# Hybrid encoder block on one core: nine matmuls of `zv` moved behind the first step of `za`, the row scale moved ahead by one table step, and the load order changed to match

## The reference, cut to what matters

```python
def _rms(x, g):
    y = xf * lax.rsqrt(jnp.mean(xf * xf, axis=-1, keepdims=True) + EPS)
    return (y * g.astype(jnp.float32)).astype(x.dtype)
...
h = _rms(x, g_mix[l])
z = h @ w_in[l]
za, zu, zv, zq, zg = jnp.split(z, SPLITS, axis=-1)
ya = jax.nn.gelu(_s5(za, ...))
yb = _sgu(zu, zv, ...)
yc = _mem_xattn(zq, mem, ...)
merged = gates[:, :, 0] * ya + gates[:, :, 1] * yb + gates[:, :, 2] * yc
x = x + merged @ w_out[l]
```

## Time and profile before

| | |
|---|---|
| median of 3 runs | 768.78 us (768.48 to 768.9) |
| the profiled execution's own time | 768.33 us |
| its span in the profile | 766.6 us |
| TensorE busy | 758.3 us, 99% of the span |
| VectorE, ScalarE, GpSimd busy | 552.5, 355.4, 314.6 us |
| mean granted TensorE clock | 0.999 of full speed |

### The profile page before, as it was taken

How to read it: one execution, slowest core, us unless ns; L and a number is a source line. 1 busy time by engine, 2 the same in 40 slices (tenths; PEclk the granted TensorE clock), 3 DMA queues, 4 the chain that set the end, 5 groups by cost and what they waited for, 6 DMA issues and landing times.

```text
span 766.6 us, 9762 instructions
## 1 busy us (share of the span) xinstructions
PE 758.3 (99%) x3562; PEld 629.0 (82%) x3562; DVE 552.5 (72%) x752; ACT 355.4 (46%) x529; POOL 314.6 (41%) x169
## 2 busy tenths in 40 slices
PE   8999999999999999999999999999999999999997
PEld 7788887788888888888888888888888888888886
DVE  6999997684848484246767787777787677836687
ACT  6796567643535333634343423232323333434554
POOL 4456655233333333444444444444444354830000
PEclk9999999999999999999999999999999999999999
DMA  7744333022222443222233866666668567768853
GB/s 273 301 147 131 117 98 112 30 91 83 81 85 68 126 144 104 83 93 100 83 111 99 272 196 228 217 217 191 201 204 285 176 218 228 264 229 279 293 201 125
DMA packets 42371, 126.17 MB, mean 165 GB/s; under 512 B 4192, under 2 KB 6368, under 8 KB 40544
## 3 DMA queue, kind: packets, MB, share of 16 engines
q1 hardware_dynamic: 42192, 125.45, 49.1%
q10 hardware_dynamic: 144, 0.26, 0.1%
HBM read 107.08 MB, written 18.61 MB: 164 GB/s over the span
## 4 chain that ended last, share of the span: by engine, by line
PE 91%; ACT 3%; DVE 3%; DMA 1%; issue 1%; SPq 0%; POOL 0%; ACTq 0%
PE bank L1641 24%; PE bank L1643 24%; PE bank L1642 24%; PE bank L2005 4%; PE bank L2007 4%; PE bank L2006 4%; ACT uc L656 1%; DVE s5p L1015 1%; PE bank L1882 1%; PE bank L1757 1%; PE bank L1774 1%; DMA xT<-xt_dram 1%; ACT w_hi L596 1%; DVE tab_tmp L1015 1%; DVE h_lo L1020 1%
## 5 line engine op out<-in xcount | busy, mean ns | idle before, releaser
L535 POOL TENSOR_TENSOR w_lo<-raw,w_hi 128x1024 fp32r<-128x1024 f32 x90 | 218.1, 2424 | 300.7 <-ACT w_hi L596 300.7
L596 ACT ACTIVATE w_hi<-raw 128x1024 fp32r<-128x1024 f32 x112 | 118.8, 1060 | 310.9 <-PE bank L1643 306.3
L1641 PE MATMUL bank<-h_hi,w_hi 128*128 128x512 f32 x608 | 238.5, 392 | 0.2 <-POOL w_lo L540 0.2
L1643 PE MATMUL bank<-h_hi,w_lo 128*128 128x512 f32 x608 | 236.7, 389 | 0.0
L1642 PE MATMUL bank<-h_lo,w_hi 128*128 128x512 f32 x608 | 236.6, 389 | 0.0
L1641 PEld LDWEIGHTS bank<-h_hi,w_hi 128*128 128x128 f32 x608 | 114.2, 188 | 24.3 <-issue 1.0
L1643 PEld LDWEIGHTS bank<-h_hi,w_lo 128*128 128x128 f32 x608 | 114.1, 188 | 23.9
L1642 PEld LDWEIGHTS bank<-h_lo,w_hi 128*128 128x128 f32 x608 | 114.2, 188 | 23.7 <-issue 0.5
L540 POOL TENSOR_TENSOR w_lo<-raw,w_hi 128x512 fp32r<-128x512 f32 x48 | 67.2, 1420 | 52.4 <-ACT w_hi L596 46.0
L1015 DVE TENSOR_TENSOR mix<-mix 128x512 f32<-128x512 f32 x44 | 47.6, 1083 | 13.1 <-DMA mix<-w_dram 11.9
L1015 DVE TENSOR_TENSOR lo<-raw,hi 128x1536 fp32r<-128x1536 f32 (+1 forms) x19 | 32.8, 1732 | 24.8 <-ACT hi L925 24.6
(11 more groups left out here) (328 smaller groups left out, 1384.6 us busy)
## 6 DMA issues: line engine op xcount, KB each, us to landing
raw<-w_dram SPq DMA_DIRECT2D x112, 512.0 KB, 3.4
mix<-w_dram SPq DMA_DIRECT2D x11, 1024.0 KB, 8.0
mix_dram<-mix SPq DMA_DIRECT2D x11, 1024.0 KB, 6.3
raw<-w_dram SPq DMA_DIRECT2D x30, 256.0 KB, 4.3
raw<-mix_dram SPq DMA_DIRECT2D x26, 256.0 KB, 3.8
half_dram<-odd SPq DMA_DIRECT2D x11, 256.0 KB, 8.3
second<-half_dram SPq DMA_DIRECT2D x3, 768.0 KB, 6.0
raw<-mix_dram SPq DMA_DIRECT2D x3, 768.0 KB, 4.2
```

The source lines that it names most:

```text
L535: nc.gpsimd.tensor_tensor(w_lo[:, s, :], raw[:, s, :], fv(w_hi[:, s, :]), ALU.subtract).then_inc(w_ready, 1)
L596: nc.scalar.activation(w_hi[:, slot, :], raw[:, slot, :], ACT.Copy).then_inc(w_rounded, 1)
L1641: mm(out, a[0], b[0], start=first, stop=False)
L1643: return mm(out, a[1], b[0], start=False, stop=last)
```

## The change

The first 512 columns of `zv`'s first weight tile (tile 4, which is one of its two steps) are loaded once more, into a buffer `raw_v` of their own, right after `x`'s first tile. ScalarE rounds them to `v_hi` behind `x`'s first tile, GpSimd subtracts them to `v_lo` behind the first half of weight tile 0, and TensorE does the nine matmuls of `zv_step(0, range(3))` behind `za_step(0)` instead of behind `za_step(7)`. Tile 4 is still loaded and rounded as a whole. In SyncE's order tile 4 now stands ahead of the fourth token tile, tile 5 ahead of `mtok`; ScalarE rounds tile 4 ahead of the fourth token square. On VectorE `x_scale` comes behind `table_step(1)`, and the copy to `rstd` ahead of `table_step(4)`; `uT` stays behind both. Some semaphores are shared (`diag`, `wide_done`, `trig_ready`).

```diff
+        raw_v = at("raw_v", o_f + 2048, [P, WB])
+        v_hi = at("v_hi", o_f + 4096, [P, WB], R)
+        v_lo = at("v_lo", o_f + 6144, [P, WB], R)
...
             for k in range(4):
                 load_first(k // 2, k % 2)
                 load_x(k)
+                if k == 0:
+                    sp.dma_start(raw_v[:, :], w_d[T_ZV, :, 0:WB]).then_inc(v_loaded, 16)
             load_x(4)
             next_weights(2)
             load_x(5)
             next_weights(3)
-            for t in range(4):
+            for t in range(3):
                 sp.dma_start(xtok[:, t, :], xtok_d[:, t, :]).then_inc(xtok_loaded[t], 16)
             next_weights(4)
+            sp.dma_start(xtok[:, 3, :], xtok_d[:, 3, :]).then_inc(xtok_loaded[3], 16)
             sp.dma_start(memf[:, :, :], mem_d).then_inc(mem_loaded, 16)
             sp.dma_start(small[:, C_BRE:N_SMALL], small_d[:, C_BRE:N_SMALL]).then_inc(small_loaded, 16)
+            next_weights(5)
             sp.dma_start(mtok[:, :, :], mtok_d).then_inc(mtok_loaded, 16)
-            for t in range(5, 8):
+            for t in range(6, 8):
                 next_weights(t)
...
                     low_half(t, j).then_inc(done, 1)
+                    if t == 0 and j == 0:
+                        pool.wait_ge(v_rounded, 1)
+                        nc.gpsimd.tensor_tensor(v_lo[:, :], raw_v[:, :], fv(v_hi[:, :]), ALU.subtract
+                                                ).then_inc(v_ready, 1)
...
                 round_first(k // 2, k % 2)
                 round_x(k)
+                if k == 0:
+                    act.wait_ge(v_loaded, 16)
+                    nc.scalar.activation(v_hi[:, :], raw_v[:, :], ACT.Copy).then_inc(v_rounded, 1)
...
             for t in range(4):
+                if t == 3:
+                    round_weights(T_ZV)
                 act.wait_ge(xtok_loaded[t], 16)
                 token_square(xtok, t, t)
             act.wait_ge(tok_sq, 4)
             root(tstd[:, :], tssq[:, 0:4]).then_inc(tok_std, 1)
-            round_weights(T_ZV)
...
-            def table_step(n, scale=None):
+            def table_step(n):
...
-                if scale:
-                    scale()
                 turn_squared(ER, EI, ER, EI)
...
             table_step(1)
-            table_step(2, x_scale)
+            x_scale()
+            table_step(2)
+            dve.wait_ge(wide_done, 1)
+            V.tensor_copy(rstd[:, :], bank[7][:, :]).then_inc(rstd_ready, 1)
             table_step(4)
-            dve.wait_ge(wide_x, 1)
-            V.tensor_copy(rstd[:, :], bank[7][:, :]).then_inc(rstd_ready, 1)
             dve.wait_ge(rstd_ready, 1)
...
-            for k in range(KD):
+            za_step(0)
+            x_hi, x_lo = h(0)
+            pe.wait_ge(v_rounded, 1)
+            for c in range(3):
+                mm(bank[4 + c][:, :], x_hi[:, c * P:(c + 1) * P], v_hi[:, :], start=True, stop=False)
+            for c in range(3):
+                mm(bank[4 + c][:, :], x_lo[:, c * P:(c + 1) * P], v_hi[:, :], start=False, stop=False)
+            pe.wait_ge(v_ready, 1)
+            for c in range(3):
+                mm(bank[4 + c][:, :], x_hi[:, c * P:(c + 1) * P], v_lo[:, :], start=False, stop=False)
+            for k in range(1, KD):
                 za_step(k)
...
-            pe.wait_ge(w_half, T_ZV + 1)
-            zv_step(0, range(3))
-            pe.wait_ge(diag_x, 1)
-            wide_rows(7, xdiag[:, :, :], T, wide_x)
+            pe.wait_ge(diag, 1)
+            wide_rows(7, xdiag[:, :, :], T, wide_done)
```

More of the change, by code:

```diff
@@ L265, in build @@
         w_used = sem("w_used")
+        v_loaded, v_rounded, v_ready = sems("v_loaded v_rounded v_ready")
         X_PARTS = ((0, 1), (1, 2), (2, 3), (3, 4), (4, 6), (6, 8))
@@ L277, in build @@
         norms = {n: dict(zip(keys, sems(" ".join(f"{n}_{k}" for k in keys)))) for n, keys in NORM_KEYS.items()}
-        tok_sq, tok_std, diag_x, diag_m, wide_x, wide_m, rstd_ready, mrstd_ready = sems(
-            "tok_sq tok_std diag_x diag_m wide_x wide_m rstd_ready mrstd_ready")
+        tok_sq, tok_std, diag, wide_done, rstd_ready, mrstd_ready = sems(
+            "tok_sq tok_std diag wide_done rstd_ready mrstd_ready")
         za_taken, zv_taken, zq_taken, k_taken, v_taken, zu_scaled, zu_ready = sems(
@@ L286, in build @@
         pt_done, pt_act, pt_dve, pv_done, o_hi_s, o_lo_s = sems("pt_done pt_act pt_dve pv_done o_hi_s o_lo_s")
-        dt_ready, ang_ready, trig_ready = sems("dt_ready ang_ready trig_ready")
+        ang_ready, trig_ready = sems("ang_ready trig_ready")
         j1_g, j1_th, j1_merge = sems("j1_g j1_th j1_merge")
@@ L623, in _ @@
             act.wait_ge(vec_loaded, 16)
-            nc.scalar.activation(s5p[:, 0, :], small[:, C_LDT:C_LDT + 16], ACT.Exp).then_inc(dt_ready, 1)
+            nc.scalar.activation(s5p[:, 0, :], small[:, C_LDT:C_LDT + 16], ACT.Exp).then_inc(trig_ready, 1)
             for k in range(4):
@@ L1027, in _ @@
             dve.wait_ge(vec_loaded, 16)
-            dve.wait_ge(dt_ready, 1)
+            dve.wait_ge(trig_ready, 1)
             go(tt(XR, are, DT, ALU.mult))
@@ L1048, in _ @@
                 low_x(k)
-            dve.wait_ge(trig_ready, 1)
+            dve.wait_ge(trig_ready, 2)
             go(tt(ARE, MAG, CS, ALU.mult))
@@ L1129, in x_scale @@
             def x_scale():
-                token_scale(4, 1, tstd[:, :], trstd[:, :], xdiag[:, :, :], diag_x)
+                token_scale(4, 1, tstd[:, :], trstd[:, :], xdiag[:, :, :], diag)
             table_step(1)
-            table_step(2, x_scale)
+            x_scale()
+            table_step(2)
+            dve.wait_ge(wide_done, 1)
+            V.tensor_copy(rstd[:, :], bank[7][:, :]).then_inc(rstd_ready, 1)
             table_step(4)
-            dve.wait_ge(wide_x, 1)
-            V.tensor_copy(rstd[:, :], bank[7][:, :]).then_inc(rstd_ready, 1)
             dve.wait_ge(rstd_ready, 1)
@@ L1144, in _ @@
                 low_tile(norms["m"], m_hi, m_lo, memf, C_GMEM, k)
-            token_scale(2, 2, mtstd[:, :], mtrstd[:, :], mdiag[:, :, :], diag_m)
+            token_scale(2, 2, mtstd[:, :], mtrstd[:, :], mdiag[:, :, :], diag)
             bre, bim, cre, cim = (grid(c0) for c0 in (C_BRE, C_BIM, C_CRE, C_CIM))
@@ L1173, in _ @@
             times([c[:, 0, :, :] for c in cpow], (cre, cim), ARE, AIM, True, 1)
-            dve.wait_ge(wide_m, 1)
+            dve.wait_ge(wide_done, 2)
             V.tensor_copy(mrstd[:, :], bank[3][:, 0:M]).then_inc(mrstd_ready, 1)
@@ L1729, in _ @@
                 if t == 3:
-                    pe.wait_ge(diag_m, 1)
+                    pe.wait_ge(diag, 2)
                     pe.wait_ge(za_taken, KB)
-                    wide_rows(3, mdiag[:, :, :], M, wide_m)
+                    wide_rows(3, mdiag[:, :, :], M, wide_done)
                 for j in range(2):
```

## The result

The change makes the kernel 0.24% slower: 770.48 us (median of 22 runs, 769.35 to 771.74) against 768.64 us for the kernel before (22 runs, 767.87 to 769.99). The ratio is 1.0024, with a 95% interval of 1.0018 to 1.0030, so about 1.8 us more.

The account below looks back on a forecast made before the run. Bound at the start, where TensorE's matmuls meet VectorE's uT followed by ScalarE at 61.42 us. A 2.1 us hold makes uT late: 768.33 + 2.1 = 770.4 profiled, plus 0.45 to the median, so 770.9 us; range 768.0 to 772.2.

Parts of the forecast that it names:

- Two paths, the later decides: At 61.42 us TensorE's matmuls meet VectorE up to uT followed by ScalarE; the later one sets the time.
- ScalarE's stretch from `uT` to the half rest: ScalarE's work from 36.91 to 59.5 has no idle stretch; if it got shorter, late uT would not reach TensorE.
- tile 5's pair: GpSimd's two subtractions for tile 5, expected to start at about 33.5, where they were.
- The hold of 2.1 us: VectorE's table step 4, behind rstd, held by GpSimd's pair for tile 5: 2.1 us, bounds 0 to 2.56; chance 0.62.
- The added load: v's extra 256 KB slice behind x's first tile: no shift taken, VectorE at most 0.64 us later.
- The table step did not get by: First rival: the third table step ends before GpSimd's pair or runs beside none, uT not held, 768.3 to 768.8; chance 0.32.
- The fourth token row: Rival: this row lands at 30.8 behind tile 4, delaying the root and uT by 4.2 us, total 773.0; chance 0.06.
- The moved matmuls did find something to fill: Third rival denied it: v's slice lands with x's second tile, TensorE's 0.7 us is lost, total stays 770.9; no chance given.
- the 0.9 that I gave its path: TensorE's path up to 61.42 becomes 0.9 us shorter: 0.7 from the moved matmuls plus 0.2 of idle.
- The 0.7 us: TensorE's gain from the moved matmuls: through at 30.3 instead of 31.03.
- The wait ahead of 61.42: TensorE's idle time before the half rest at 61.42, taken as 0.2 us.
- 771.3: The total by the skill page's blocking rule, each subtraction holding VectorE for its whole length: 768.78 + 2.56.

Follow-up runs that it names:

- e1: The changed kernel with only table_step(4) moved behind the four uT: 768.41 us against 768.56 for the kernel before, ratio 0.9997.
- e5: The kernel before, with the copy of rstd and the four uT put ahead of table_step(4): 768.56 us against 768.59, ratio 1.0003.
- e6: The changed kernel with VectorE's old order (scale behind table_step(2), copy of rstd behind table_step(4)): 769.23 us, ratio 1.0015 to the kernel before.
- e4: The changed kernel with token rows and tile 4's rounding in the old order and table_step(4) behind uT: 767.47 us against 768.56 before, ratio 0.9986.
- e0_change_a: The changed kernel, unaltered, run once more for another profile: 769.63 us, one execution.

## Why the prediction was right

**Two paths, the later decides.** Right, and shown from both sides: with `uT` late the time follows it one for one (the table), with `uT` early TensorE's own path is met (e1, e5). ScalarE's stretch from `uT` to the half rest kept its length, 22.7 us (37.90 to 60.62, 36.91 to 59.58 in the earlier trace rows); it was the point on which everything could have failed.

**The terms.** Predicted and measured, in the first profile of the change:

| step | predicted | measured |
|---|---|---|
| nine matmuls | 9.23 to 11.27 | 9.23 to 11.29 |
| TensorE through `za` | 30.3 | 30.48 (30.65 less 0.17 idle) |
| tile 3 rounded from | 19.5 | 19.70 |
| tile 4 rounded from | 24.9 | 25.14 |
| fourth token square from | 26.1 | 26.83 |
| `tok_std` | 28.9 | 29.6 |
| tile 5's pair from | 33.5 | 33.93 |
| copy of `rstd` done | 32.65 | 32.75 |
| table step behind it, hold | 2.1 | 1.0 (1.1 and 2.1 in the two other executions) |
| last `uT` done | 39.0 | 37.9 (38.2 and 39.2) |

ScalarE's rows behind the second half of the table:

```profile
25.14 1.06 ACT L609 ACTIVATE w_hi<-raw 128x1024 fp32r<-128x1024 f32 x1 [1.26 <-PE bank L1715]
26.83 1.06 ACT L631 ACTIVATE xtok<-xtok 128x1024 f32<-128x1024 f32 x1 [0.62 <-DMA xtok<-xtok_dram]
...
29.29 0.30 ACT L618 ACTIVATE tstd<-tssq,eps 128x4 f32<-128x4 f32 x1
...
32.81 1.05 ACT L609 ACTIVATE w_hi<-raw 128x1024 fp32r<-128x1024 f32 x1
```

The fourth square waits 0.62 us for its row, which I had put at 25.9 and which came at 26.8. In the two other executions the square starts at 26.22 and 26.12, as predicted. The late row passes on to the root, but not to `rstd`: by the sum itself VectorE came to the scale only at 29.4, 0.5 us behind the root. It idled 0.29 us there and made most of it up in the scale and table step 2.

**The mis-sized term.** The hold of 2.1 us, taken from the earlier trace rows, is right for an execution in which both of GpSimd's subtractions catch the step, and twice too large where only one does. In three profiles it was 1.0, 1.1 and 2.1. The prediction had one held subtraction only as the low end of its range. Which case comes up follows the start of tile 5's pair (33.93 and 34.36: one; 33.25: two), and that follows ScalarE's eight `m_hi`: they began at 29.59 and 30.02, in the first case behind the late row, in the second after waiting 1.04 us for the memory's rows, and at 28.92 in the third. So the execution whose token and memory rows came most punctually lost the most. The 22 runs lie between 769.35 and 771.74, where one and two holds (+1.0 and +2.1 on 768.64) would put most of them. The median, 770.48, lies near the execution with two holds (770.60), and only one of the 22 is below the second execution with one (769.63). That each timed run has one or two holds is an inference, since only three were traced. Of the 0.4 us by which 770.9 is too high, 0.14 is the base (768.78 from three runs, 768.64 from 22); the rest is this term, 1.84 in the medians for 2.1.

**The added load.** Taken at nothing, with a bound of 0.64 us. `h_hi` of `x`'s second tile started at 8.64, 8.54 and 9.30 in the three executions (8.73 before), so in one of them 0.6 us late. Nearly all of that was made up on the way: the copy of `rstd` started at 32.06, 32.26 and 32.30.

**The rivals.** The table step did not get by in any of the three executions of the change; e6, where GpSimd's pair came as late as 34.85, shows that it can. The fourth token row was late by under 1 us and not by the 4 that this rival needs, and e1 shows no loss with the row still behind tile 4. The late loads are not free, though: e4 gains over e1, e6's chain runs through them, and in the change ScalarE was through the memory's squares only at 37.1, so that without a hold too tile 6 would have begun 0.2 us later than in the earlier trace rows. The moved matmuls did find something to fill: with the hold gone, e1 has TensorE at 60.48, 0.94 us earlier than the earlier trace rows, for the 0.9 that I gave its path. In the change all of it is swallowed. The sum agrees better than its parts, which is in part luck. The 0.7 us compares a start-to-start pace (30.3) with the end of a last matmul (31.03); measured alike, 31.03 became 30.48, which is 0.55. In e1 TensorE then waits 0.51 us for the diagonal, whose matmul comes only 0.43 earlier (30.96). The wait ahead of 61.42 in turn was worth 0.4 and not 0.2: that matmul starts 0.52 us after the one ahead of it (60.90), and in e1 0.12 (60.36, 60.48).

**Where the gain went.** Of e1's 0.94 us only 0.56 is left in its profiled execution's own time (767.77 for 768.33), and 0.15 in the medians. In e4, 1.69 us at TensorE become 1.24 (767.09). Some 0.4 us is given back behind the start in both, and all of it at one later half rest. Before, the matmul behind that rest starts at 78.21, 0.12 us after the one ahead of it. In e1 it is 0.49 (77.13, 77.62) and in e4 0.51 (76.41, 76.92). VectorE, the chain and TensorE of e1 there:

```profile
75.03 1.29 DVE L1032 TENSOR_TENSOR cpow<-pow_tmp 128x512 f32<-128x512 f32 x2
...
75.77 1.72 POOL w_lo L549
...
77.62 0.47 PE L1657 MATMUL bank<-h_hi,w_hi 128*128 128x512 f32 x1 [0.22 <-POOL w_lo L549]
```

GpSimd's subtraction takes 1.72 us, where half a pair is about 1.28. The second of VectorE's two `cpow` instructions had begun before it. That fits the same hold with the roles exchanged; no run here tests it.

## What to carry to other kernels

Two engines that work side by side without a semaphore can still be ordered by a resource that they share, and an instruction far above the usual time of its shape is the sign of it. Before a step is moved, one should look at what the other engine does at its new place, and lay work that was not held (here what reads PSUM) under the other's stretch; e4 gains 1.1 us by that, where the same edits without it lose 2.1. A path with slack takes any shortening without a trace, so gains have to be made on both paths at once.

## What the runs showed of the hardware

The opening says that the engines meet only at semaphores and that all instructions of a table step read two operands in SBUF. The traces show otherwise on both points: VectorE and GpSimd also hold each other up without a semaphore, and the last instruction of each step, a copy, reads one operand. A held VectorE instruction ends about 0.1 us or less behind GpSimd's subtraction, however small it is: of a pair of 2.54 us (33.25 to 35.79, about 1.27 each) one product was stretched to end at 34.62 and the sum behind it to end at 35.88. One instruction can go by between the two subtractions (the copy of 0.16 at 35.19). The Trainium skill, page "SBUF — State Buffer", section "Who interferes with whom", has the later of the two blocked for the whole of the other; the trace agrees for each subtraction by itself, but not for the 2.56 us of the whole pair, by which the prediction had worked out 771.3 (1.0 or 2.1 us were lost, and the median is 770.48). I had not expected that an instruction with one SBUF input would be held too; the copy of 128 x 16 elements, elsewhere 0.17 us, was held in both further executions of the change (1.29 us at 34.39, and 1.27 at 26.06). VectorE of e0_change_a, whose pair for tile 5 starts at 34.36:

```profile
34.39 1.29 DVE L1101 COPY s5p<-s5p 128x16 f32<-128x16 f32 x1
35.71 2.48 DVE L1032 TENSOR_TENSOR uT<-bank,rstd 128x512 f32<-128x512 f32 x4
```

The instructions with a PSUM input kept their time in every profile: 0.69 for the copy of `rstd` and 2.48 for the four `uT`, under GpSimd's pair as beside it.
